# Order of a chunk pair's matmuls: high weights of both chunks, then low weights of both

## The chip, the cores and the metric

The kernel runs on one core of one Trainium2 chip. The metric is the device time of one execution in microseconds; lower is better.

## What is computed

Two transformer layers over 256 tokens of width 2048, all in float32. The first has sparse attention (compressed, selected and window branches, 16 heads in 4 groups) and a gated feed-forward of inner width 5632; the second has an mLSTM branch (8 heads), a pooling branch and a gated merge. Cut to the large products, with `@` a matrix product:

```python
h = x + nsa_mixer(rmsnorm(x, g0), ...)          # h @ w_in (q, k, v), attention, @ w_out
h = h + swiglu(rmsnorm(h, g1), w_in, w_out)     # (silu(a) * b) @ w_out
x = rmsnorm(h, g2)
proj = einsum('bsd,de->bse', _rmsnorm(x, w), w_in_2)   # q, k, v, o, z, gates, pool, merge gates
...                                             # causal conv, mLSTM, pooling
out = (sigmoid(g_a) * br_a + sigmoid(g_b) * br_b) @ w_out_2
x = x + _rmsnorm(out, norm_post_w)
```

Nearly all of the arithmetic is 256 rows times weight matrices. The weights are read once each, 387 MB in all.

## The kernel before

**Stream.** The weights lie in DRAM as 730 chunks of 128 partitions x 1024 floats (512 KB), in the order of use. Chunk c passes through slot c % 4 of a ring (`RING = 4`). SyncE loads it into `raw[slot]`. ScalarE (`split`, L435 to L442) copies it to `w_hl[slot][:, 0]` in the type fp32r, which keeps the high part of each number, and raises `hi_ready`. VectorE (`split`, L711 to L717) subtracts that from `raw` and writes the rest, the low part, to `w_hl[slot][:, 1]`, raising `lo_ready`. ScalarE may overwrite a slot only when TensorE has raised `chunks_done` for the chunk that was in it four chunks before. Both engines run three chunks ahead (`AHEAD = 3`).

**Products.** The activations are split in the same way (`x_hl`, `f_hl`, `o_hl`, `ya_hl`, `m_hl`: index 0 high, 1 low). A block of 512 output columns is two units, each of 256 columns with its own PSUM pair `sets[0]` or `sets[1]`. A unit is 4 chunks for an inner width of 2048 (`n // 2` with `n = NB = 8`), 11 for the second product of the feed-forward (`ND = 22`), 2 for the pooling branch's product. In `unit_features` (L1367) one chunk holds four 128-row tiles of the inner dimension by two of the output. Its first half are 8 matmuls of the high weights against high and low activations side by side, 512 columns each (L1373); its second half, behind a wait for `lo_ready`, are 8 matmuls of the low weights against the high activations, 256 columns each (L1378). `unit_tokens` (L1382) has the roles exchanged: it waits for `lo_ready` at its start, because its 8 matmuls of 512 columns (L1388) stream high and low weights side by side, and its 8 of 256 columns (L1391) need the high ones alone.

**Units and steps.** `gemm` (L1412) runs two units, `unit` (L1402) the chunks of one. `unit` also takes `steps`, small pieces of other work on TensorE that are put behind a chunk by its number within the block: the attention's score matmuls behind chunks 0, 2, 4, 6 and its value matmuls and transposes behind 1, 3, 5, 7 (`attention`, L1548); parts of the mLSTM heads (L1709 to L1713); row statistics (L1454). VectorE and ScalarE have such steps of their own between their `split`s, in the order in which the Python loops write them; each engine works in that order.

**Attention on TensorE.** `scores(gi, n)` (L1508) writes banks `m[0]` and `m[1]`. VectorE's `mask_scores` (L897) reads both, adds the bias, finds the maxima and raises `masked` with its last operation (L924). `values(gi, n)` (L1534) writes `m[1]` again, so it waits for the masks of the head two further on, which is the head whose scores stand behind the chunk just before:

```python
            if n + 2 < HPG:
                pe.wait_ge(masked, gi * HPG + (n + 3))
```

The groups gi = 0, 1, 2 run as `steps` of a `gemm` (L1563 to L1565). Group 3 runs in a loop over chunks of `block_features` (L1573), which doesn't go through `unit`.

**mLSTM heads.** In the block of the gate z (`ml_block(i, 5)`, L1712) TensorE sums squares of head 0 behind chunk 2 and of head 1 behind chunk 5 (`head_squares`, L1703). VectorE's order there is: low parts, `head_var(0)` (L1237) behind the split of the fourth turn, another split, `take_z` (L1260) at half, `head_sum(1)` (L1232), on which `head_squares(1)` waits. There are four such blocks (i = 0 to 3).

**Inputs of a block.** With `ready`, a chunk also waits until the activations that it reads are there: chunk j of the first unit waits for `x_ready` 4j + 4.

Of the kernel before, what the change touches and what calls it, by code (L numbers as in the profile page):

```python
# [13 lines left out]
P = 128  # L14
S = 256
# [19 lines left out]
HB, HT = BLK // 2, FT // 2  # L35
# [105 lines left out]
def program(nc, d):  # L141
# [108 lines left out]
    sets = [ctx.enter_context(nc.psum_tensor(f"set{n}", [P, 2 * BLK], F32)) for n in range(2)]  # L250
# [6 lines left out]
    hi_ready, lo_ready = sem("hi_ready"), sem("lo_ready")  # L257
    chunks_done = sem("chunks_done")
# [1068 lines left out]
    def _(pe):  # L1327
        mm = nc.tensor.matmul
# [38 lines left out]
        def unit_features(at, j, out, hl, kts, first):  # L1367

            w = w_hl[at.slot(j)]
            tiles = [(k, kt, f) for k, kt in enumerate(kts) for f in range(HT)]  # L1370
            for k, kt, f in tiles:
                c = slice(k * HB + f * P, k * HB + (f + 1) * P)
                mm(out[:, f * 2 * S:(f + 1) * 2 * S], w[:, 0, c], hl[:, kt, :, :], start=first and k == 0, stop=False,  # L1373
                   skip_group_check=True)
            pe.wait_ge(lo_ready, at.at(j) + 1)
            for k, kt, f in tiles:
                c = slice(k * HB + f * P, k * HB + (f + 1) * P)
                last = mm(out[:, f * 2 * S + S:(f + 1) * 2 * S], w[:, 1, c], hl[:, kt, 0, :], start=False, stop=True,  # L1378
                          skip_group_check=True)
            return last  # L1380

        def unit_tokens(at, j, out, hl, kts, first):  # L1382

            w = w_hl[at.slot(j)]
            tiles = [(k, kt, t) for k, kt in enumerate(kts) for t in range(TT)]
            pe.wait_ge(lo_ready, at.at(j) + 1)
            for k, kt, t in tiles:
                mm(out[:, t * 2 * HB:(t + 1) * 2 * HB], hl[:, kt, 0, t * P:(t + 1) * P], w[:, :, k * HB:(k + 1) * HB],  # L1388
                   start=first and k == 0, stop=False, skip_group_check=True)
            for k, kt, t in tiles:  # L1390
                last = mm(out[:, t * 2 * HB + HB:(t + 1) * 2 * HB], hl[:, kt, 1, t * P:(t + 1) * P],  # L1391
                          w[:, 0, k * HB:(k + 1) * HB], start=False, stop=True, skip_group_check=True)
            return last

        def chunk(at, j, wait, emit):

            pe.wait_ge(hi_ready, at.at(j) + 1)
            if wait:
                pe.wait_ge(*wait)
            emit().then_inc(chunks_done, 1)  # L1400

        def unit(at, j0, number, the_set, n, ready, hl, emit, steps):  # L1402

            await_set(number)
            for j in range(n):
                kts = range(4 * j, 4 * j + 4)
                chunk(at, j0 + j, ready(kts[-1]) if ready else None,
                      lambda: emit(at, j0 + j, sets[the_set % 2], hl, kts, j == 0))
                if steps and j0 + j in steps:
                    steps[j0 + j]()  # L1410

        def gemm(at, number, the_set, n=NB, ready=None, hl=x_hl, emit=(unit_features, unit_features), steps=None):  # L1412

# [38 lines left out]
        for n in range(4):  # L1452
            gemm(Pos(C_KV + n * NB), B_KV + 2 * n, B_KV, ready=operand_ready(0) if n == 0 else None,
                 steps={1: relative, 6: lambda: stats(0, 0, 1)} if n == 0 else None)  # L1454
        for n in range(2):
            await_set(B_KV + 8 + n)
            at = Pos(C_KV + (4 + n) * NB)
# [12 lines left out]
        for n in range(2):  # L1470
            await_set(B_CMP + n)
            out = sets[(B_CMP + n) % 2][0:GROUPS * NC, 0:2 * CH]
            at = Pos(C_CMP + n * NB)
            pe.wait_ge(blk_ready, n + 1)
            for j in range(NB):
                pe.wait_ge(lo_ready, at.at(j) + 1)
                w = w_hl[at.slot(j)]
                for k in range(4):
                    kt, c = 4 * j + k, slice(k * CH, (k + 1) * CH)
                    mm(out, blk_hi[:, n, kt, :], w[:, :, c], start=kt == 0, stop=False, skip_group_check=True)  # L1480
                    last = mm(out[:, CH:2 * CH], blk_lo[:, n, kt, :], w[:, 0, c], start=False, stop=kt == CB - 1,
                              skip_group_check=True)
# [89 lines left out]
        at, slot = Pos(C_OUT), 0  # L1572
        for block_no, j0, count in ((0, 0, 6), (1, 0, 6), (0, 6, 2), (1, 6, 2)):  # L1573
            for j in range(j0, j0 + count):
                kts = (2 * j, 2 * j + 1)
# [295 lines left out]
```

## Time and profile before

| | us |
|---|---|
| median of 3 runs | 2188.57 (2186.68 to 2189.26) |
| profiled execution | 2188.28 |
| its span, first to last instruction | 2186.6 |
| TensorE busy | 2159.9 (99%) |
| VectorE busy | 1414.4 (65%) |
| ScalarE busy | 1049.6 (48%) |
| DMA queue of the weights, share of 16 engines | 54.1% |

Between the span and the time of the same execution lie 1.7 us that no instruction covers. TensorE's duration of one matmul overlaps the next one's, so the pace is read from the starts: a row of the time line gives the start of a run of equal instructions, how long the run lasted and how many it has.

### The profile page before, as it was taken

To read this page: it belongs to the slowest core of one execution; us is meant where nothing else is said; L and a number is where in the kernel's file an instruction comes from. 1 tells how busy PE (TensorE), PEld (TensorE's weight loads), DVE (VectorE), ACT (ScalarE), POOL (GpSimd) and SP (SyncE) were. 2 spreads that over 40 slices of the span, in tenths; PEclk is the share of its full clock that TensorE was granted. 3 is DMA by queue.
4 is the path that set the end of the run, shared out by engine and by line. 5 is a ranking of instruction groups with operands and counts; after the bars stand their busy time and mean duration, and the time that the engine had idled before them with its cause. 6 is when DMAs were issued, how large, how long until landed. Compare 5 with 4: busy or idle time off the path is not lost.

```text
span 2186.6 us, 34436 instructions
## 1 busy us (share of the span) xinstructions
PE 2159.9 (99%) x12438; PEld 1891.5 (87%) x12438; DVE 1414.4 (65%) x1839; ACT 1049.6 (48%) x1373; POOL 70.5 (3%) x143
## 2 busy tenths in 40 slices
PE   9999999999999999999999999999999999999996
PEld 8877889888888888888888888888888888888885
DVE  7756664766666656655556677867777676566565
ACT  5445554454444444444444455444454454444453
POOL 1000322000000000000000000000000000000001
PEclk9999999999999999999999999999999999999998
DMA  7557333556565655555555456545555555555552
GB/s 277 185 189 244 117 127 117 179 172 200 180 196 178 195 188 186 190 190 187 188 190 191 145 174 193 180 168 184 187 177 177 171 185 190 184 192 189 186 191 97
DMA packets 108598, 395.54 MB, mean 181 GB/s; under 512 B 12307, under 2 KB 12323, under 8 KB 108513
## 3 DMA queue, kind: packets, MB, share of 16 engines
q1 hardware_dynamic: 106272, 386.97, 54.1%
q0 software_dynamic: 2096, 7.33, 1.0%
q8 instruction: 61, 1.00, 0.2%
q14 instruction: 25, 0.20, 0.0%
q10 hardware_dynamic: 144, 0.04, 0.0%
HBM read 389.83 MB, written 2.13 MB: 179 GB/s over the span
## 4 chain that ended last, share of the span: by engine, by line
PE 95%; DVE 1%; ACT 1%; DMA 1%; issue 0%; SPq 0%; POOL 0%; ACTq 0%
PE set L1373 52%; PE set L1378 27%; PE set L1388 4%; PE set L1391 2%; PE set L1362 1%; PE set L1364 1%; PE set L1363 1%; PE misc L1544 1%; ACT w_hl L442 1%; PE set L1348 1%; PE set L1350 1%; PE set L1349 1%; PE misc L1530 1%; DMA h<-in_x 0%; PE misc L1679 0%; PE misc L1546 0%
## 5 line engine op out<-in xcount | busy, mean ns | idle before, releaser
L717 DVE TENSOR_TENSOR w_hl<-raw,w_hl 128x1024 fp32r<-128x1024 f32 x730 | 888.0, 1225 | 586.0 <-ACT w_hl L442 579.0
L442 ACT ACTIVATE w_hl<-raw 128x1024 fp32r<-128x1024 f32 x730 | 762.2, 1055 | 799.9 <-PE set L1378 693.7
L1373 PE MATMUL set<-x_hl,w_hl 128*128 128x512 f32 x3584 | 908.1, 395 | 0.0
L1373 PEld LDWEIGHTS set<-x_hl,w_hl 128*128 128x128 f32 x3584 | 646.7, 189 | 118.7 <-issue 1.4
L1378 PEld LDWEIGHTS set<-x_hl,w_hl 128*128 128x128 f32 x3584 | 490.0, 191 | 35.4
L1378 PE MATMUL set<-x_hl,w_hl 128*128 128x256 f32 x3584 | 500.5, 283 | 0.0
L1373 PE MATMUL set<-f_hl,w_hl 128*128 128x512 f32 x704 | 176.3, 392 | 0.0
L449 ACT ACTIVATE cross<-set 128x512 f32<-128x512 f32 (+1 forms) x152 | 88.5, 583 | 138.2 <-PE set L1378 126.7
L1373 PEld LDWEIGHTS set<-f_hl,w_hl 128*128 128x128 f32 x704 | 126.6, 189 | 22.6
L1378 PEld LDWEIGHTS set<-f_hl,w_hl 128*128 128x128 f32 x704 | 96.0, 190 | 6.9
L1378 PE MATMUL set<-f_hl,w_hl 128*128 128x256 f32 x704 | 98.2, 282 | 0.0
L1388 PE MATMUL set<-w_hl,x_hl 128*128 128x512 f32 x384 | 96.2, 392 | 0.0
L1388 PEld LDWEIGHTS set<-w_hl,x_hl 128*128 128x128 f32 x384 | 69.1, 189 | 12.4
L1373 PE MATMUL set<-ya_hl,w_hl 128*128 128x512 f32 x256 | 64.1, 392 | 0.0
L1373 PE MATMUL set<-m_hl,w_hl 128*128 128x512 f32 x256 | 64.1, 392 | 0.0
L1391 PEld LDWEIGHTS set<-w_hl,x_hl 128*128 128x128 f32 x384 | 52.4, 190 | 3.7
L1391 PE MATMUL set<-w_hl,x_hl 128*128 128x256 f32 x384 | 53.5, 282 | 0.0
L1373 PEld LDWEIGHTS set<-ya_hl,w_hl 128*128 128x128 f32 x256 | 46.0, 189 | 8.2
L1373 PEld LDWEIGHTS set<-m_hl,w_hl 128*128 128x128 f32 x256 | 46.0, 189 | 8.2
L400 POOL TENSOR_TENSOR prob<-prob,share 128x128 f32<-128x128 f32 (+1 forms) x96 | 38.0, 428 | 115.0 <-DVE share L935 115.0
L1167 DVE SCALAR_TENSOR_TENSOR t<-cq,cur,t 128x256 f32<-128x256 f32 x96 | 40.0, 479 | 0.0
L526 ACT ACTIVATE prob<-prob,ntop 128x128 f32<-128x128 f32 (+1 forms) x96 | 37.4, 390 | 0.0
(294 smaller groups left out, 1764.0 us busy)
## 6 DMA issues: line engine op xcount, KB each, us to landing
raw<-in_weights SPq DMA_DIRECT2D x730, 512.0 KB, 4.1
bias_g<-bias POOLq DMA_DIRECT2D x4, 572.0 KB, 3.8
cur<-in_cur POOLq DMA_DIRECT2D x4, 535.0 KB, 3.9
h<-in_x SPq DMA_DIRECT2D x4, 512.0 KB, 8.4
bias<-u_dram POOLq DMA_DIRECT2D x1, 2048.0 KB, 14.4
out<-y_t SPq DMA_DIRECT2D x4, 512.0 KB, 2.8
w<-in_w POOLq DMA_DIRECT2D x1, 256.0 KB, 6.6
vm<-in_causal POOLq DMA_DIRECT2D x1, 192.0 KB, 3.1
```

The costliest lines, as they stand in the source:

```text
L400: last = g.tensor_tensor(pr[:, lo:lo + w], pr[:, lo:lo + w], sh[:, b, t:t + 1].to_broadcast([P, w]), ALU.mult)
L442: a(w_hl[at.slot(j)][:, 0, :], raw[at.slot(j)][:, :], ACT.Copy).then_inc(hi_ready, 1)
L449: a(dst, src, ACT.Copy).then_inc(crossed, 1)
L526: last = a(pr[:, lo:lo + w], pr[:, lo:lo + w], ACT.Exp, bias=ntop[:, b, t:t + 1], accum_out=total[n % 2][:, b, t:t + 1])
L717: tt(w_hl[s][:, 1, :], raw[s][:, :], w_hl[s][:, 0, :].bitcast(F32), ALU.subtract).then_inc(lo_ready, 1)
L1167: last = stt(t1[:, f, :], cq[:, f, k:k + S], cur[:, c + k:c + k + 1], t1[:, f, :], ALU.mult, ALU.add)
L1348: mm(o, w[:, 0, c], hl[:, kt, 0, :], start=starts, stop=False, skip_group_check=True)
L1349: mm(o, w[:, 0, c], hl[:, kt, 1, :], start=False, stop=False, skip_group_check=True)
L1373: mm(out[:, f * 2 * S:(f + 1) * 2 * S], w[:, 0, c], hl[:, kt, :, :], start=first and k == 0, stop=False, skip_group_check=True)
L1378: last = mm(out[:, f * 2 * S + S:(f + 1) * 2 * S], w[:, 1, c], hl[:, kt, 0, :], start=False, stop=True, skip_group_check=True)
L1388: mm(out[:, t * 2 * HB:(t + 1) * 2 * HB], hl[:, kt, 0, t * P:(t + 1) * P], w[:, :, k * HB:(k + 1) * HB], start=first and k == 0, stop=Fals ...
L1391: last = mm(out[:, t * 2 * HB + HB:(t + 1) * 2 * HB], hl[:, kt, 1, t * P:(t + 1) * P], w[:, 0, k * HB:(k + 1) * HB], start=False, stop=Tru ...
```

## The change

The two halves of a chunk become two functions, `high` and `low`. `unit` takes its chunks in pairs: the high halves of both, then the low halves of both. A chunk's `chunks_done` and its step come after its own low half. A unit of 11 chunks has five pairs and a single one. The number and kind of matmuls stay; each chunk keeps its waits for `hi_ready`, `ready` and `lo_ready`, ahead of the half that needs them. (In `unit_tokens` the wait for `hi_ready` is gone, that for `lo_ready` stays.) `block_features`, `block_tokens`, `narrow` and the compression loop are as before.

```diff
--- before.py
+++ after.py
@@ -1368,29 +1368,42 @@
 
             w = w_hl[at.slot(j)]
             tiles = [(k, kt, f) for k, kt in enumerate(kts) for f in range(HT)]
-            for k, kt, f in tiles:
-                c = slice(k * HB + f * P, k * HB + (f + 1) * P)
-                mm(out[:, f * 2 * S:(f + 1) * 2 * S], w[:, 0, c], hl[:, kt, :, :], start=first and k == 0, stop=False,
-                   skip_group_check=True)
-            pe.wait_ge(lo_ready, at.at(j) + 1)
-            for k, kt, f in tiles:
-                c = slice(k * HB + f * P, k * HB + (f + 1) * P)
-                last = mm(out[:, f * 2 * S + S:(f + 1) * 2 * S], w[:, 1, c], hl[:, kt, 0, :], start=False, stop=True,
-                          skip_group_check=True)
-            return last
+
+            def high():
+                pe.wait_ge(hi_ready, at.at(j) + 1)
+                for k, kt, f in tiles:
+                    c = slice(k * HB + f * P, k * HB + (f + 1) * P)
+                    mm(out[:, f * 2 * S:(f + 1) * 2 * S], w[:, 0, c], hl[:, kt, :, :], start=first and k == 0, stop=False,
+                       skip_group_check=True)
+
+            def low():
+                pe.wait_ge(lo_ready, at.at(j) + 1)
+                for k, kt, f in tiles:
+                    c = slice(k * HB + f * P, k * HB + (f + 1) * P)
+                    last = mm(out[:, f * 2 * S + S:(f + 1) * 2 * S], w[:, 1, c], hl[:, kt, 0, :], start=False, stop=True,
+                              skip_group_check=True)
+                last.then_inc(chunks_done, 1)
+
+            return high, low
 
         def unit_tokens(at, j, out, hl, kts, first):
 
             w = w_hl[at.slot(j)]
             tiles = [(k, kt, t) for k, kt in enumerate(kts) for t in range(TT)]
-            pe.wait_ge(lo_ready, at.at(j) + 1)
-            for k, kt, t in tiles:
-                mm(out[:, t * 2 * HB:(t + 1) * 2 * HB], hl[:, kt, 0, t * P:(t + 1) * P], w[:, :, k * HB:(k + 1) * HB],
-                   start=first and k == 0, stop=False, skip_group_check=True)
-            for k, kt, t in tiles:
-                last = mm(out[:, t * 2 * HB + HB:(t + 1) * 2 * HB], hl[:, kt, 1, t * P:(t + 1) * P],
-                          w[:, 0, k * HB:(k + 1) * HB], start=False, stop=True, skip_group_check=True)
-            return last
+
+            def high():
+                pe.wait_ge(lo_ready, at.at(j) + 1)
+                for k, kt, t in tiles:
+                    mm(out[:, t * 2 * HB:(t + 1) * 2 * HB], hl[:, kt, 0, t * P:(t + 1) * P], w[:, :, k * HB:(k + 1) * HB],
+                       start=first and k == 0, stop=False, skip_group_check=True)
+
+            def low():
+                for k, kt, t in tiles:
+                    last = mm(out[:, t * 2 * HB + HB:(t + 1) * 2 * HB], hl[:, kt, 1, t * P:(t + 1) * P],
+                              w[:, 0, k * HB:(k + 1) * HB], start=False, stop=True, skip_group_check=True)
+                last.then_inc(chunks_done, 1)
+
+            return high, low
 
         def chunk(at, j, wait, emit):
 
@@ -1402,12 +1415,18 @@
         def unit(at, j0, number, the_set, n, ready, hl, emit, steps):
 
             await_set(number)
-            for j in range(n):
-                kts = range(4 * j, 4 * j + 4)
-                chunk(at, j0 + j, ready(kts[-1]) if ready else None,
-                      lambda: emit(at, j0 + j, sets[the_set % 2], hl, kts, j == 0))
-                if steps and j0 + j in steps:
-                    steps[j0 + j]()
+
+            for pair in range(0, n, 2):
+                js = range(pair, min(pair + 2, n))
+                parts = [emit(at, j0 + j, sets[the_set % 2], hl, range(4 * j, 4 * j + 4), j == 0) for j in js]
+                for j, (high, low) in zip(js, parts):
+                    if ready:
+                        pe.wait_ge(*ready(4 * j + 3))
+                    high()
+                for j, (high, low) in zip(js, parts):
+                    low()
+                    if steps and j0 + j in steps:
+                        steps[j0 + j]()
 
         def gemm(at, number, the_set, n=NB, ready=None, hl=x_hl, emit=(unit_features, unit_features), steps=None):
```

## Rows read from the trace of the kernel before

**Rows 1.** The page: TensorE's busy time, and the ending chain by line
```profile
PE 2159.9 (99%) x12438; PEld 1891.5 (87%) x12438; DVE 1414.4 (65%) x1839; ACT 1049.6 (48%) x1373; POOL 70.5 (3%) x143
...
PE set L1373 52%; PE set L1378 27%; PE set L1388 4%; PE set L1391 2%; PE set L1362 1%; PE set L1364 1%; PE set L1363 1%; PE misc L1544 1%; ACT w_hl L442 1%; PE set L1348 1%; PE set L1350 1%; PE set L1349 1%; PE misc L1530 1%; DMA h<-in_x 0%; PE misc L1679 0%; PE misc L1546 0%
```

**Rows 2.** Waits: engine, line, releaser; total us, times, longest us
```profile
PE misc L1530 <- POOL prob L400: 1.8, 1, 1.8
PE misc L1446 <- DVE stat L778: 1.5, 1, 1.5
...
PE set L1373 <- ACT w_hl L442: 0.2, 1, 0.2
...
ACT w_hl L442 <- PE set L1378: 693.7, 427, 7.0
```

**Rows 3.** Time line of TensorE, one chunk: start, us, engine, line, operation, count
```profile
1003.16 2.00 PE L1373 MATMUL set<-f_hl,w_hl 128*128 128x512 f32 x8
1005.00 1.12 PE L1378 MATMUL set<-f_hl,w_hl 128*128 128x256 f32 x8
1005.95 2.00 PE L1373 MATMUL set<-f_hl,w_hl 128*128 128x512 f32 x8
```

**Rows 4.** Time line of TensorE in a block of `block_tokens`, 512-column matmuls alone
```profile
138.44 0.39 PE L1362 MATMUL set<-w_hl,x_hl 128*128 128x512 f32 x1
...
143.20 0.39 PE L1362 MATMUL set<-w_hl,x_hl 128*128 128x512 f32 x1
```

**Rows 5.** Time line, fourth chunk of the mLSTM part's first block
```profile
1180.44 3.50 DVE L717 TENSOR_TENSOR w_hl<-raw,w_hl 128x1024 fp32r<-128x1024 f32 x3 [2.93 <-ACT w_hl L442]
...
1181.93 2.00 PE L1388 MATMUL set<-w_hl,x_hl 128*128 128x512 f32 x8
```

**Rows 6.** Time line, the first chunk of the kernel
```profile
9.48 2.07 PE L1373 MATMUL set<-x_hl,w_hl 128*128 128x512 f32 x8
...
10.49 1.69 DVE L747 SCALAR_TENSOR_TENSOR x_hl<-h,gains,x_hl 128x256 fp32r<-128x256 f32 x4 [0.27 <-ACT x_hl L465]
...
11.40 1.11 PE L1378 MATMUL set<-x_hl,w_hl 128*128 128x256 f32 x8
```

**Rows 7.** Stretches: us, busy PE, PEld, DVE, ACT, POOL, PEclk, DMA share, GB/s
```profile
28.00:33.00 5.00, 3.46 (x22) 2.95 (x20) 4.90 (x6) 3.20 (x3) 0.00 (x0) 1.00 0.87 320
33.00:36.50 3.50, 3.50 (x11) 2.76 (x11) 3.35 (x4) 0.08 (x1) 0.00 (x0) 0.53 1.01 369
...
220.00:224.00 4.00, 2.18 (x14) 1.94 (x15) 3.97 (x5) 2.59 (x6) 3.68 (x5) 1.00 0.30 116
```

**Rows 8.** Time line, attention group 1: behind the scores of one head
```profile
246.63 2.09 PE L1373 MATMUL set<-x_hl,w_hl 128*128 128x512 f32 x8
...
247.02 0.25 DVE L910 TENSOR_TENSOR prob<-misc,bias_g 128x15 f32<-128x15 f32 x2
...
248.56 1.11 PE L1378 MATMUL set<-x_hl,w_hl 128*128 128x256 f32 x8
248.63 0.64 DVE L924 TENSOR_SCALAR ntop<-top 128x6 f32<-128x6 f32 x1
...
249.51 0.59 PE L1544 MATMUL misc<-prob_t,v_g 128*128 128x256 f32 x2
```

**Rows 9.** The last operation of the masks: duration ns min/median/max, starts
```profile
L924 DVE TENSOR_SCALAR ntop<-top x16: 172/514/640, 212.0 to 358.0; 128x6 f32<-128x6 f32 x16
```

**Rows 10.** Time line, block of the gate z, i = 1
```profile
1460.94 0.60 PE L1707 MATMUL misc<-t,ones 128*128 128x256 f32 x2
...
1462.23 1.23 DVE L717 TENSOR_TENSOR w_hl<-raw,w_hl 128x1024 fp32r<-128x1024 f32 x1 [2.29 <-ACT w_hl L442]
...
1463.83 1.75 DVE L1240 RECIPROCAL stat<-stat 128x256 f32<-128x256 f32 x1
...
1467.92 0.42 DVE L1235 TENSOR_TENSOR t<-t 128x256 f32<-128x256 f32 x1
...
1469.75 0.60 PE L1707 MATMUL misc<-t,ones 128*128 128x256 f32 x2
```

## Prediction

> **What bounds the kernel now.** I read the page first: TensorE is busy for 2159.9 of 2186.6 us, and the chain that ended last runs through its two matmul lines, L1373 and L1378, for 79% of the span [rows 1]. So the kernel is bound by TensorE's stream, and there are three ways to change its time: the pace inside the stream, the few holes in it, and new holes. The waits come second. TensorE's own are few: 1.8 us for the probabilities of the first head, 1.5 us for the first row statistics, 0.2 us at one chunk of the out projection [rows 2]. ScalarE waits for TensorE 427 times, 693.7 us in all [rows 2]; the splits are far ahead, held back by the ring. The time line comes third. A chunk is 8 matmuls of 512 columns in 1.84 us (1003.16 to 1005.00) and 8 of 256 in 0.95 us, 2.79 us together [rows 3]. I call them the high and the low run.
>
> **Pace of the stream.** In `block_tokens`, where only 512-column matmuls follow each other, 21 of them take 4.76 us (138.44 to 143.20), 0.2267 us each, with chunk waits between them [rows 4]. At that pace 8 take 1.813 us; the high run takes 1.84 [rows 3]. So a high run that follows a low run has about 0.027 us that a high run behind another high run should not have. The low run doesn't show such an excess: 0.95 us for 8, 0.119 each. Rounding is 0.01 us on each side, and a long low run may be slower by that much a pair. I take 0.02 us saved per pair, between 0.027 and 0.017. The units have 680 chunks, of which 8 are the single last chunks of units of 11; 336 pairs. 336 x 0.02 = 6.7 us gained (5.7 to 9.1; 0 if the excess doesn't hang on the change of width, and then the low run's loss of up to 3.4 us is left).
>
> The Trainium skill says otherwise ("TensorE: Matmul & The Clock Gate", Back-to-back issue gap): the gap of warm matmuls hangs on their columns alone, N/2.4 + 2.5 ns. By it the order is worth nothing, and the sum below would be 6.7 us higher; rows 3 against rows 4, 230 ns and 227 ns for the same 512 columns, don't agree with it.
>
> **The ring.** The first chunk of a pair now reports `chunks_done` one high run, 1.84 us, later, so its successor in the slot is split later by that; the second reports as before, but its high run is wanted one low run, 0.95 us, earlier. From a chunk's report to the use of its successor in the slot are three chunks, 8.4 us [rows 3]; a split takes 1.2 us on VectorE [rows 5, 10], about as much ahead of it on ScalarE, and ScalarE has idle time of its own, 1.6 us per wait (693.7 us over 427) [rows 2]. Some 5 us of room hide 1.84 and 0.95. SyncE's loads wait for `lo_ready`, which is early too. Zero, save where a split is late today:
> - The out projection's chunk with the 0.2 us wait [rows 2] is the fourth of its block, the second of a pair. Its split comes when it came; TensorE asks 0.95 us sooner: +0.9 us.
> - The fourth chunk of the mLSTM part is of `unit_tokens`, whose high run needs the low part. VectorE ends the first of three splits at 1180.44 + 1.17 = 1181.61, TensorE starts at 1181.93 [rows 5]. Wanted 0.95 us sooner, at 1180.98, it comes 0.63 us late, and I add 0.15 for the semaphore and the weight load: +0.8 us.
> - At the start, the second chunk needs the second four activation tiles, ready at 10.49 + 1.69 = 12.18; the first high run ends at 11.40 [rows 6]. Today the low run lies between: 0.78 us and a weight load, +0.85 us.
>
> **Steps behind odd-numbered chunks** (the second of a pair) keep their place. Those behind even-numbered ones move behind the partner's high run, 1.84 us later. For a step that waited this is a gain: the row statistics stand behind chunk 6, and their wait of 1.5 us [rows 2] is covered if VectorE's squares don't move as much. VectorE is busy for 4.90 of the 5 us before them [rows 7], so it is late by its own work and not for TensorE's reports; I take the whole 1.5. After that wait TensorE's granted clock fell, 0.53 on average over 33.0 to 36.5 [rows 7], its lower level of 1.2 GHz for most of the stretch, which costs 3.5 x 0.47 = 1.6 us. I count it as gone with the gap ahead of it: together -3.1 us (0 at worst).
>
> **Attention, the largest term.** `scores(n)` is behind an even-numbered chunk, `values(n - 2)` behind the odd one next to it, and values wait for the masks of head n, made from those scores (both use bank `m[1]`). Today a high and a low run lie between scores and values; after the change only the low run. The row: the high run behind the scores starts at 246.63, VectorE begins the masks at 247.02 and ends them at 248.63 + 0.64 = 249.27; the values start at 249.51 [rows 8]. So the masks end 2.64 us after TensorE has left the scores, and the cover is 2.88 us, hardly more. With a low run alone it is 0.95 us, plus about 0.08 for the change from the scores' operand type, which the high run shows here (1.93 us, 246.63 to 248.56, instead of 1.84). The wait in this head is 2.64 + 0.1 (weight load ahead of the matmul, estimated) - 1.03 = 1.7 us; its last operation took 0.64 us where the median of 16 is 0.51 [rows 9], so I take 1.6 for the mean head. No other work is behind the wait but the transposes and the next pair, all on TensorE. How many: groups 1 and 2 have four each, group 0 the last two (its first slots have no head to finish), group 3 runs outside `unit`. 10 x 1.6 = 16 us lost; with the shortest and the longest of that operation, 0.17 and 0.64, 10 x 1.25 to 10 x 1.7. VectorE can't start sooner, because the scores are later by the same 1.84 us, and what it does in between was done before them. The next exponentials start behind transposes, as today. The only wait for the probabilities now is that of the first head [rows 2], and that chain isn't lengthened, so nothing further adds.
>
> **The gate z's blocks.** `head_squares(0)` is behind chunk 2 and moves 1.84 us. `head_var(0)` on VectorE is also behind the low part of chunk 6, which waits for chunk 2's `chunks_done`. Today that split starts at 1462.23, `head_var` ends at 1463.83 + 1.75 = 1465.58, then follow a split and `take_z`, `head_sum(1)` ends at 1467.92 + 0.42 = 1468.34, and TensorE takes it at 1469.75, 1.4 us later [rows 10]. The chain begins with chunk 2's report and is back to back but for short gaps, so it moves by nearly the whole 1.84 us, to about 1470.2, while TensorE arrives when it did, 1469.7 with the faster runs: with the weight load a wait of 0.7 us in each of the 4 blocks, 2.8 us (0 where the gaps take up the shift, 5 at twice 0.7). Behind it are only TensorE's own matmuls.
>
> **Sum.** -6.7 - 3.1 + 0.85 + 0.9 + 0.8 + 16 + 2.8 = +11.5 us. On the profiled execution's 2188.28 us, of which 1.7 lie outside the span, that is 2199.8; the median of the runs is 0.3 higher: 2200.
>
> **Rivals.**
> - *Clock drops* (chance 0.14). The new holes are 1.6 us, ten of them 11 us apart. One hole of 1.5 us was followed by a stretch at half clock; the one of 1.8 us in the first attention group was not, the granted clock is 1.00 over 220 to 224 [rows 7]. If four of the ten cost 1.6 us each, the time is 2206; if all, 2216.
> - *The excess of the high run stays* (0.14). It may belong to the place of the weights in the chunk and not to the change of width; rows 4 are another kind of block, which speaks for this. Then 6.7 us of gain are missing, and up to 3.4 us are lost on the low runs: 2207 to 2210. The rule of the skill's page named above, by which no order of matmuls costs more than another, ends at the lower of the two, 2207.
> - *The masks are hidden after all* (0.08; the other side). If TensorE's queue delays the low run, or VectorE ends the masks 1.6 us sooner, the 16 us vanish. Then -9.8 + 2.55 + 2.8 = -4.5 us is left: 2184, faster. It decides at a masks' time of 1.04 us behind the scores, against 2.64 measured; nothing in the rows speaks for it but that the profile shows ends of matmuls by a model. Half way the result is no change, 2189 to 2193 (0.10).
> - My forecast, 2195 to 2204: 0.54.
>
> The range leaves out the faster case (0.08), the lower part of the half way (0.03) and the far part of the clock's and of the second rival's (0.07): 2190 to 2210. A measurement of this kernel can tell about 0.2%, 4.4 us. Chances: slower by more 0.82, within it 0.10, faster 0.08.
>
> **What would show it.** In the profile after, the waits of TensorE should have a new row, L1544's operation released by VectorE's L924, ten times, 1.6 us at most each; without it the largest term is wrong. The row for the first statistics should be gone, and the clock at full speed behind it. Four waits on L1235 of about 0.7 us should be at the squares of the second head. The time line of a pair in the feed-forward should show 16 matmuls of 512 columns in about 3.66 us and 16 of 256 in 1.91, 5.57 together instead of 5.59. A longer low run, or a high run of 3.68, would show the second rival. Half-clock stretches between 230 and 330 us would show the first.

## The result and the profile after

The changed kernel takes 2196.2 us (median of 7 runs, 2193.51 to 2198.64); the kernel before, timed beside it, 2187.9 (7 runs, 2185.85 to 2189.27). The ratio is 1.0039, with a 95% interval of 1.0029 to 1.0049: slower by 8.3 us. The forecast was 2200.0 with a range of 2190 to 2210, and slower. The profiled execution took 2196.38 us.

The page of the kernel after: span, busy time of the engines, and the chain that ended last by line, which answers to [rows 1].

```profile
span 2193.9 us, 34360 instructions
...
PE 2154.9 (98%) x12438; PEld 1891.1 (86%) x12438; DVE 1392.9 (63%) x1839; ACT 1031.4 (47%) x1373; POOL 70.9 (3%) x143
...
PE set L1376 52%; PE set L1383 26%; PE set L1397 4%; PE set L1402 2%; DVE w_hl L717 1%; PE misc L1563 1%; ACT w_hl L442 1%; PE set L1362 1%; PE set L1363 1%; PE set L1364 1%; PE set L1348 1%; PE set L1350 1%; PE set L1349 1%; PE misc L1549 1%; PE misc L1698 0%
```

The high and low runs are L1376 and L1383 now (L1373 and L1378 before). TensorE is busy for 5.0 us less and the span is 7.3 us longer: the stream got shorter, and holes were added. Which ones, the waits of TensorE say (line, releaser; total us, times, longest), against [rows 2]:

```profile
PE misc L1563 <- DVE ntop L924: 8.4, 9, 1.0
...
PE set L1376 <- DVE x_hl L747: 1.5, 1, 1.5
PE misc L1726 <- DVE t L1235: 1.3, 4, 0.4
...
PE set L1376 <- ACT w_hl L442: 1.2, 1, 1.2
PE set L1376 <- DVE t L1078: 1.1, 1, 1.1
PE misc L1563 <- issue: 1.0, 1, 1.0
PE misc L1549 <- POOL prob L400: 0.8, 1, 0.8
...
PE set L1397 <- DVE w_hl L717: 0.7, 1, 0.7
```

L1563 is the first value matmul of a head (L1544 before). It waits ten times; nine are put down to the masks, the tenth, which is the first in time, to "issue", for which the profile names no releaser; its masks end 0.15 us ahead of it. The 1.5 us of the first row statistics are gone. A wait on L1078 is there that the prediction doesn't have.

One head of attention group 1 in the time line, which answers to [rows 8]:

```profile
245.02 1.11 PE L1383 MATMUL set<-x_hl,w_hl 128*128 128x256 f32 x8
...
245.82 2.25 POOL L400 TENSOR_TENSOR prob<-prob,share 128x128 f32<-128x128 f32 x6 [6.72 <-DVE share L935]
...
247.25 1.19 PE L1383 MATMUL set<-x_hl,w_hl 128*128 128x256 f32 x8
247.53 0.25 DVE L910 TENSOR_TENSOR prob<-misc,bias_g 128x15 f32<-128x15 f32 x2 [1.80 <-PE misc L1539]
...
249.14 0.17 DVE L924 TENSOR_SCALAR ntop<-top 128x6 f32<-128x6 f32 x1
...
249.37 0.70 PE L1563 MATMUL misc<-prob_t,v_g 128*128 128x256 f32 x2 [0.93 <-DVE ntop L924]
```

Only the low run at 247.25 lies between the scores and the values. The masks start 0.28 us behind the scores and end at 249.31; TensorE stands idle for 0.93 us.

Pairs in the feed-forward's second product, which answer to [rows 3]:

```profile
999.83 2.08 PE L1383 MATMUL set<-f_hl,w_hl 128*128 128x256 f32 x16
1001.74 3.82 PE L1376 MATMUL set<-f_hl,w_hl 128*128 128x512 f32 x16
1005.39 2.08 PE L1383 MATMUL set<-f_hl,w_hl 128*128 128x256 f32 x16
1007.31 3.82 PE L1376 MATMUL set<-f_hl,w_hl 128*128 128x512 f32 x16
```

A pair is 5.57 us (1001.74 to 1007.31). By the starts in nanoseconds its median is 5567 (3654 high, 1912 low, over 246 pairs); a chunk of the kernel before is 2793 (1841 and 952, over 548), two of them 5586. A pair saves 19 ns.

The place of every microsecond comes from the times at which TensorE reports the same chunk in both traces (the last matmul of a chunk). The table gives, for each stretch, the kernel's duration less that of the kernel before, in us. x1 to x8 are the experiments below, without x4, which leaves work out.

| stretch | after | x1 | x2 | x3 | x5 | x6 | x7 | x8 |
|---|---|---|---|---|---|---|---|---|
| chunks 1 and 2 | +0.91 | -0.11 | +1.08 | +0.85 | +0.13 | +0.92 | -0.09 | +0.15 |
| chunks 3 to 16 (first statistics) | -3.52 | -1.63 | -3.52 | -3.52 | -3.37 | -3.52 | -1.63 | -3.45 |
| rest of keys and values | -0.16 | 0 | -0.16 | -0.16 | 0 | -0.16 | 0 | -0.16 |
| compression, first block of queries | +0.22 | +0.78 | +0.34 | +0.13 | -0.43 | -0.01 | -0.88 | -0.04 |
| attention group 0 | +0.14 | +0.01 | +0.31 | +0.25 | 0 | +0.14 | -1.05 | +0.32 |
| groups 1, 2, and the step behind 2's last chunk | +10.48 | 0 | 0 | +1.66 | 0 | +10.52 | 0 | 0 |
| out projection, third block | +0.94 | 0 | +0.93 | +0.94 | 0 | +0.93 | 0 | 0 |
| out projection, fourth block | -0.08 | 0 | -0.08 | -0.08 | 0 | -0.08 | 0 | -0.08 |
| feed-forward, first product | -1.76 | -1.76 | -1.76 | -1.76 | 0 | -1.76 | +14.61 | -1.76 |
| feed-forward, second product | -0.80 | -0.80 | -0.80 | -0.80 | 0 | -0.80 | -0.80 | -0.80 |
| mLSTM i = 0, first block | +0.87 | 0 | +0.88 | +0.88 | 0 | +0.87 | 0 | 0 |
| its second block | +0.85 | 0 | +0.85 | +0.87 | 0 | +0.85 | 0 | 0 |
| its next three | -0.23 | 0 | +1.40 | -0.25 | -1.51 | +1.42 | 0 | +1.37 |
| its gate z | +0.57 | 0 | +0.57 | +0.57 | 0 | 0 | 0 | 0 |
| i = 1 to 3 | +0.33 | 0 | +0.33 | +0.33 | 0 | -1.20 | 0 | -1.24 |
| merge, last product | -1.44 | -1.44 | -1.44 | -1.44 | 0 | -1.44 | -1.44 | -1.44 |

Where pairs alone act, the table is -0.020 us for each: 1.76 over 88, 1.12 over 56. The first row also holds the moment at which TensorE begins, which differs between traces by more than 0.1 us. Groups 1 and 2 of attention lose 4.66 and 4.63 us for four waits each (the rest of 10.48 is the step behind group 2's last chunk): with 0.08 for their four pairs, 1.19 a wait. (The profile's 0.9 to 1.0 counts only from the modelled end of the matmul before, and the end overlaps the next start.)

### The profile page after: what moved, and what is told of

Its sections match the earlier page's. It is cut to its first block, busy times and chain, and to the rows that moved or that the text cites. A ratio compares the mean times of both kernels' runs of the same rounds, so it can differ in the third digit from the quotient of the medians.

```text
span 2193.9 us, 34360 instructions
## 1 busy us (share of the span) xinstructions
PE 2154.9 (98%) x12438; PEld 1891.1 (86%) x12438; DVE 1392.9 (63%) x1839; ACT 1031.4 (47%) x1373; POOL 70.9 (3%) x143
## 4 chain that ended last, share of the span: by engine, by line
PE 94%; DVE 3%; ACT 1%; issue 1%; DMA 1%; POOL 0%; SPq 0%; DVEq 0%; ACTq 0%
PE set L1376 52%; PE set L1383 26%; PE set L1397 4%; PE set L1402 2%; DVE w_hl L717 1%; PE misc L1563 1%; ACT w_hl L442 1%; PE set L1362 1%; PE set L1363 1%; PE set L1364 1%; PE set L1348 1%; PE set L1350 1%; PE set L1349 1%; PE misc L1549 1%; PE misc L1698 0%
## 5 line engine op out<-in xcount | busy, mean ns | idle before, releaser
L717 DVE TENSOR_TENSOR w_hl<-raw,w_hl 128x1024 fp32r<-128x1024 f32 x730 | 876.2, 1225 | 671.0 <-ACT w_hl L442 666.2
L442 ACT ACTIVATE w_hl<-raw 128x1024 fp32r<-128x1024 f32 x730 | 745.9, 1056 | 894.7 <-PE set L1383 798.3
L1376 PE MATMUL set<-x_hl,w_hl 128*128 128x512 f32 x3584 | 861.6, 392 | 2.6 <-DVE x_hl L747 1.5
L1376 PEld LDWEIGHTS set<-x_hl,w_hl 128*128 128x128 f32 x3584 | 659.9, 188 | 133.2 <-DVE x_hl L747 2.8
L1383 PEld LDWEIGHTS set<-x_hl,w_hl 128*128 128x128 f32 x3584 | 462.1, 191 | 18.4 <-issue 0.7
L1383 PE MATMUL set<-x_hl,w_hl 128*128 128x256 f32 x3584 | 472.3, 284 | 0.0
L1376 PE MATMUL set<-f_hl,w_hl 128*128 128x512 f32 x704 | 168.7, 391 | 0.0
L1376 PEld LDWEIGHTS set<-f_hl,w_hl 128*128 128x128 f32 x704 | 129.1, 188 | 24.8
L1383 PEld LDWEIGHTS set<-f_hl,w_hl 128*128 128x128 f32 x704 | 90.8, 191 | 3.7
L1397 PE MATMUL set<-w_hl,x_hl 128*128 128x512 f32 x384 | 91.8, 391 | 0.7 <-DVE w_hl L717 0.7
L1383 PE MATMUL set<-f_hl,w_hl 128*128 128x256 f32 x704 | 91.9, 283 | 0.0
L1376 PE MATMUL set<-ya_hl,w_hl 128*128 128x512 f32 x256 | 61.1, 391 | 0.0
L1376 PE MATMUL set<-m_hl,w_hl 128*128 128x512 f32 x256 | 61.1, 391 | 0.0
L1376 PEld LDWEIGHTS set<-m_hl,w_hl 128*128 128x128 f32 x256 | 47.1, 188 | 9.1
L1376 PEld LDWEIGHTS set<-ya_hl,w_hl 128*128 128x128 f32 x256 | 47.1, 188 | 9.1
L400 POOL TENSOR_TENSOR prob<-prob,share 128x128 f32<-128x128 f32 (+1 forms) x96 | 37.0, 418 | 117.6 <-DVE share L935 117.6
```

What stands on the lines that cost most here:

```text
L400: last = g.tensor_tensor(pr[:, lo:lo + w], pr[:, lo:lo + w], sh[:, b, t:t + 1].to_broadcast([P, w]), ALU.mult)
L442: a(w_hl[at.slot(j)][:, 0, :], raw[at.slot(j)][:, :], ACT.Copy).then_inc(hi_ready, 1)
L717: tt(w_hl[s][:, 1, :], raw[s][:, :], w_hl[s][:, 0, :].bitcast(F32), ALU.subtract).then_inc(lo_ready, 1)
```

## The experiments

Two theories stood against each other behind the sum. Mine: the change is a small uniform gain of the stream (0.02 us a pair) plus a few holes, each at one named step that lost its cover. The rival: the order of the halves costs or gives something everywhere (through the ring, the pace, the clock), and the named steps are a part of it only. The kernel before took 2186.95 us beside x1 to x4 (27 runs) and 2186.87 beside x5 to x8 (10 runs).

**Pairs only where no step stands between** (x1). `unit` gets its group size as a parameter, 1 by default; 2 in both products of the feed-forward, the merge and the last product, 200 pairs.

```diff
-            for pair in range(0, n, 2):
-                js = range(pair, min(pair + 2, n))
+            for pair in range(0, n, group):
+                js = range(pair, min(pair + group, n))
```

> Pairs only in blocks without steps between chunks: the feed-forward's two products, the merge and the last projection, 200 pairs; every other unit takes its chunks one by one as before. Theory (a high run behind another high run lacks the excess of 0.027 us, the low run loses about 0.007): 200 x 0.02 = 4.0 us faster than before, 2184, no wait in TensorE's list that before doesn't have. Rival (the order of matmuls is worth nothing, the time by columns alone): the time of before, 2188. Second rival (the ring has less room and costs something): slower than before.

Measured: 2184.74 us (11 runs), ratio to before 0.9989 (0.9980 to 0.9998). In the trace the four stretches are shorter by 1.76, 0.80, 1.12 and 0.32, 4.00 in all, and no wait came with them: TensorE's wait for the statistics is as before. So this part of the change alone makes the kernel faster. The medians differ by 2.2 us where 4.0 was expected; the interval reaches from 0.4 to 4.4. The clock brought what the prediction didn't have (columns as in [rows 7]):

```profile
28.00:33.00 5.00, 3.52 (x22) 3.02 (x21) 4.90 (x7) 3.09 (x3) 0.00 (x0) 1.00 0.86 279
33.00:36.50 3.50, 3.50 (x20) 3.03 (x20) 3.18 (x3) 0.25 (x1) 0.00 (x0) 1.00 1.02 369
165.00:170.00 5.00, 3.14 (x15) 1.97 (x14) 2.78 (x3) 4.33 (x6) 0.00 (x0) 0.83 0.80 259
```

The same hole of 1.5 us is there (TensorE busy for 3.52 of the 5 us), and the granted clock behind it is 1.00, not 0.53; a lower one stands at 165 us instead, where the kernel before has none.

**Attention chunk by chunk, the rest as in the change** (x2): `group=1` in the two calls of `gemm` that carry the attention's steps.

> The changed kernel, but in the three blocks that carry the attention's steps the chunks run one by one. Theory (the attention's waits on the masks are the bulk of the loss): the nine waits on L924 are gone, 10.9 us less than the changed kernel, 2185, which is 2 to 3 us below before. Rival (the time was lost all over, through the ring): at most 2 us less than the changed kernel, 2194.

Measured: 2186.97 us (10 runs), ratio 0.9997 (0.9987 to 1.0006). All waits on L924 are gone, and groups 1 and 2 take what they took before, to 0.01 us. So the attention's waits account for the slowdown of the whole kernel. The expectation of 2 to 3 us below before is not borne out by the medians, which are equal; the interval reaches from 2.8 us below to 1.3 above.

**A head's scores one run earlier** (x3). In the attention's blocks the step of a pair's first chunk stands behind that chunk's high run; the partner's high run and the low run then lie between scores and values again.

```diff
                     high()
+                    if j0 + j in early:
+                        steps[j0 + j]()
...
-                    if steps and j0 + j in steps:
+                    if steps and j0 + j in steps and j0 + j not in early:
```

> The changed kernel, but in the attention blocks the step of a pair's first chunk runs behind its high run instead of its low run. Between scores and values then lie a high and two low runs, 3.7 us, against masks of 1.8 to 2.6 us. Theory (it is the distance from scores to values that costs): no wait on L924, about 10.9 us less than the changed kernel, 2185, equal to the single chunks within 0.5 us. Rival (the waits come from less room in the ring or from VectorE's work between): waits on L924 stay and the time is over 2190.

Measured: 2187.39 us (10 runs), ratio 1.0000 (0.9991 to 1.0010). Two rows of its waits, and its row for the last operation of the masks, which answers to [rows 9]:

```profile
PE misc L1539 <- DVE q_t L790: 1.0, 1, 1.0
...
PE misc L1539 <- DVE o_hl L947: 0.5, 3, 0.2
...
L924 DVE TENSOR_SCALAR ntop<-top x16: 172/335/656, 209.6 to 357.2; 128x6 f32<-128x6 f32 x16
```

No wait for the masks is left, though the attention still runs in pairs. It is the distance between scores and values that counts, as the prediction had it, not the pairs as such. The scores now sometimes stand too early for their own operands. The wait on L790 is in group 0; groups 1 and 2, with the step behind them, lose 1.66 us in place of 10.48, of which 0.5 are the three waits on L947 and the rest stays open.

**The kernel before, with five of POOL's six scalings of a head left out** (x4; the probabilities are then not all scaled). It asks what holds back the masks' last operation.

```diff
-                for b, t, lo, w in ((1, 0, O_SEL, P), (1, 1, O_SEL + P, S), (0, 0, O_CMP, NC),
-                                    (0, 1, O_CMP + 16, NC), (2, 0, O_WIN, P), (2, 1, O_WIN + P, S)):
+                for b, t, lo, w in ((0, 1, O_CMP + 16, NC),):
```

> The kernel before, with five of the six multiplications left out by which POOL scales each head's probabilities (so the output isn't the reference's). Theory (VectorE's L924 waited until POOL's multiplications had ended, as it ends 0.03 us behind them in every head): L924 takes 0.17 us in all heads instead of 0.51 in the median, the masks end 2.15 us after the scores instead of 2.5, and the first head's wait of TensorE, 1.8 us, is gone; 2186. Rival (L924 waits for its own operand on VectorE): L924 stays at 0.5 us.

Its lines are one lower from there on: L923 is L924, L399 is L400.

```profile
L923 DVE TENSOR_SCALAR ntop<-top x16: 171/172/175, 209.8 to 353.8; 128x6 f32<-128x6 f32 x16
...
L399 POOL TENSOR_TENSOR prob<-prob,share x16: 203/214/216, 216.3 to 362.0; 128x15 f32<-128x15 f32 x16
```

The operation takes 0.17 us in all 16 heads; [rows 9] has 0.51 for the median. So its length was a wait for POOL. By the single records of the kernel before, it ends 0.03 us behind POOL's last multiplication in 14 heads; in the second head it takes 0.27 us and ends 0.03 us behind the fifth of six. So it waits for the one multiplication that is running, 0.2 to 0.6 us long, and not for all of them. (The first head has none beside it. TensorE's wait for the first head's probabilities, 1.8 us in [rows 2], is gone with it; its one execution took 2184.14 us.) In the head of [rows 8] this row of the kernel before says the same:

```profile
247.00 2.24 POOL L400 TENSOR_TENSOR prob<-prob,share 128x128 f32<-128x128 f32 x6 [6.99 <-DVE share L935]
```

POOL ends at 249.24, the masks' last operation at 249.27. After the change POOL starts 1.4 us ahead of the later scores (245.82 against 247.25 above), is done by 248.07, and the operation takes 0.17. The Trainium skill ("SBUF — State Buffer", Who interferes with whom) counts `tensor_scalar`, which L924 is, among the operations that can take the port pair that VectorE and GpSimd share, and has one engine block while the other holds it. Both rows agree.

**The kernel before with the statistics one chunk later** (x5).

```diff
-                 steps={1: relative, 6: lambda: stats(0, 0, 1)} if n == 0 else None)
+                 steps={1: relative, 7: lambda: stats(0, 0, 1)} if n == 0 else None)
```

> The kernel before, with one edit: the first row statistics stand behind chunk 7 instead of chunk 6. No chunk runs in pairs. If the 1.5 us by which TensorE waited there were work of VectorE that comes when it comes, the chunk of 2.79 us between hides it: the wait's row is gone and the eighth chunk's report comes 1.5 us sooner. If VectorE's squares moved with TensorE, the wait would stay. On the clock: if the hole alone calls the half-clock stretch behind it, the clock is 1.00 from 28 to 40 us and the gain is 3.1 us; if it comes in either case it is at another place in that part of the kernel, and the gain is 1.5.

Measured: 2183.11 us, one execution. The wait is gone, and chunks 3 to 16 take 3.37 us less, where x1, with the hole but with full clock, takes 1.63 less. The difference, 1.7 us, is the hole with what is beside it; the 1.63 is the clock, since x1 has full speed there where before has not. The second gain of 1.51 us, in the mLSTM part, is also the clock: at the same place the kernel before is granted 0.83 over 10 us.

```profile
28.00:33.00 5.00, 5.00 (x30) 4.37 (x29) 4.90 (x6) 3.25 (x3) 0.00 (x0) 1.00 0.93 314
33.00:36.50 3.50, 3.50 (x23) 3.11 (x22) 3.42 (x4) 0.09 (x2) 0.00 (x0) 1.00 1.01 366
1235.00:1245.00 10.00, 10.00 (x61) 8.86 (x59) 7.36 (x13) 5.10 (x6) 0.00 (x0) 1.00 0.37 128
```

This edit has nothing to do with the mLSTM part, 1200 us later. So neither stretch at half clock can be put down to an edit from one trace of each kernel. Its time from one execution is not a measurement of the 1.5 us. The four timed executions of the kernel before with the same mean clock, 0.997, took 2183.6 to 2185.4 us.

**The gate z chunk by chunk, the rest as in the change** (x6): `group=1` in that call.

> The kernel after, with the four blocks of the gate z chunk by chunk again. My theory: their squares of head 1 wait because the report of chunk 2 comes 1.84 us later. Then the waits on L1235 are gone and each of the four blocks is 0.59 us shorter (0.67 for the wait and its weight load, less 0.08 for the four pairs given up), 2.3 us together. The rival: the wait comes from the other pairs ahead of the block, which shift VectorE's work; then waits of about 0.3 us stay and the blocks only get longer by 0.08 each.

Measured: 2195.78 us, one execution. No wait on L1235 is left. The first gate z is 0.58 us shorter than in the kernel after (+0.57 to 0), those of i = 1 to 3 1.53 together (+0.33 to -1.20), 2.1 us in all. Expected were 2.3. My account held. The +1.42 in "its next three" is once more half clock that this trace has and that of after has less of.

**Groups of four** (x7): x1, with `group=4` in the first product of the feed-forward.

> Pairs only where no step stands between them (first product of the feed-forward, second product, merge, last product), and in the first product of the feed-forward, 176 chunks, groups of four: four high runs, then four low runs. If what a pair saves is the one change from 256 to 512 columns, at 0.020 us, four chunks have one change instead of two: the first product is 44 x 0.02 = 0.9 us shorter than with pairs, 2.6 us shorter than before. The rival is the ring: the first chunk's report comes 5.5 us later than chunk by chunk, and its successor is wanted 2.9 us after it; a high split on ScalarE takes 1.06 us, so the high runs shouldn't wait, but if loads or VectorE's low parts come late, waits on L442 or L717 appear and the stretch is longer than with pairs.

Measured: 2197.03 us, one execution; that product takes 14.6 us more than before, 16.4 more than with pairs. The rival was right. The wait, and the time line around one of the twelve:

```profile
PE set L1376 <- ACT w_hl L442: 12.5, 12, 1.8
...
569.40 2.98 ACT L442 ACTIVATE w_hl<-raw 128x1024 fp32r<-128x1024 f32 x3 [6.69 <-PE set L1383]
...
572.08 5.63 PE L1376 MATMUL set<-x_hl,w_hl 128*128 128x512 f32 x24
...
576.71 1.06 ACT L575 ACTIVATE f_hl<-f_b 128x1024 f32 x1 [3.75 <-DVE f_b L1020]
577.67 1.04 ACT L442 ACTIVATE w_hl<-raw 128x1024 fp32r<-128x1024 f32 x1
...
578.76 2.11 PE L1376 MATMUL set<-x_hl,w_hl 128*128 128x512 f32 x8 [1.05 <-ACT w_hl L442]
```

ScalarE gets three slots from 569.40 on and splits them. Before the fourth its program puts the output of the block just finished (L575), which waits 3.75 us for VectorE; the fourth split ends at 578.71, and TensorE has run out after three high runs. Such a group takes 12.43 to 13.34 us. My expectation counted the split's 1.06 us and not what stands ahead of it. The pace is as expected only in part: of 43 groups 21 take 11.113 us from high run to high run, against 11.134 for two pairs, a further 0.021 for one change of width less; twelve have the wait, and the other ten take 11.13 without one, which stays open.

x7 is x1 word for word up to the feed-forward, and still it differs in the first head of attention. Two rows of x1, then two of x7:

```profile
217.50 3.31 POOL L400 TENSOR_TENSOR prob<-prob,share 128x128 f32<-128x128 f32 x6 [18.86 <-DVE share L935]
...
219.12 2.77 DVE L717 TENSOR_TENSOR w_hl<-raw,w_hl 128x1024 fp32r<-128x1024 f32 x2
```

```profile
215.85 2.25 POOL L400 TENSOR_TENSOR prob<-prob,share 128x128 f32<-128x128 f32 x6 [18.86 <-DVE share L935]
...
217.47 3.05 DVE L717 TENSOR_TENSOR w_hl<-raw,w_hl 128x1024 fp32r<-128x1024 f32 x2
```

By the single records five of the six multiplications are alike. The last begins 0.02 us behind VectorE's split (L717) in both. In x1 it takes 1.66 us and the split 1.21; in x7 it takes 0.61 and the split 1.71. So either can be the one that is held, and TensorE waits 1.8 us in x1 and 0.8 in x7. The kernel before, x2, x5 and x8 have it as x1.

The same 1.0 us is in the comparison of before and after (1.8 in [rows 2], 0.8 above), but there it comes another way:

```profile
215.91 2.25 POOL L400 TENSOR_TENSOR prob<-prob,share 128x128 f32<-128x128 f32 x6 [16.98 <-DVE share L935]
216.46 0.25 DVE L910 TENSOR_TENSOR prob<-misc,bias_g 128x15 f32<-128x15 f32 x2 [0.64 <-PE misc L1539]
...
218.44 2.71 DVE L717 TENSOR_TENSOR w_hl<-raw,w_hl 128x1024 fp32r<-128x1024 f32 x2
```

After the change the scores come later, so the masks begin 0.55 us behind POOL's start, and POOL is done at 218.16, before the split begins. That speaks for the 1.0 us being a gain of the change that the prediction doesn't have; no run tests it by itself, and x7 shows that the old order sometimes has it too.

**Pairs wherever they brought no wait** (x8): 292 pairs, and the statistics as in x5. The first block, the attention, the third block of the out projection, the gate z and the first two blocks of mLSTM i = 0 go chunk by chunk.

```diff
-                 steps={1: relative, 6: lambda: stats(0, 0, 1)} if n == 0 else None)
+                 steps={1: relative, 7: lambda: stats(0, 0, 1)} if n == 0 else None,
+                 group=1 if n == 0 else 2)
...
-            gemm(Pos(C_OUT, n, NB), B_OUT + 2 * n - 2, B_OUT, hl=o_hl)
+            gemm(Pos(C_OUT, n, NB), B_OUT + 2 * n - 2, B_OUT, hl=o_hl, group=n - 1)
-                 ready=operand_ready(2 * KT) if first else None, steps={5: norms} if first else None)
+                 ready=operand_ready(2 * KT) if first else None, steps={5: norms} if first else None, group=1 if first else 2)
```

> Pairs wherever no wait came from them: the two feed-forward products, merge, last product, the second to fourth blocks of keys and values, the first block of queries, the fourth of the out projection, and the mLSTM blocks other than the gate z's (in i = 0 not its first two), 292 pairs. Chunk by chunk: first block, attention, third block of the out projection, gate z. The first row statistics stand behind chunk 7. Theory: every pair is worth 0.020 us whatever stands between, and the waits come only from the five places named: 5.8 + 1.5 = 7.3 us below before, ratio 0.9967, about 2179.6 on a median of 2187. The rival, that each step between pairs costs something of its own, ends at pairs in the plain blocks alone, 4.0 + 1.5 = 5.5 us below, or worse.

Measured: 2179.96 us (6 runs, 2179.41 to 2181.96), ratio 0.9970 (0.9957 to 0.9982): 6.9 us below before, where 7.3 was expected, and by the two ratios some 15 below the kernel after. Its span, and its waits at the stream's lines and in attention:

```profile
span 2179.5 us, 34360 instructions
...
PE misc L1553 <- POOL prob L400: 1.8, 1, 1.8
...
PE set L1376 <- ACT w_hl L442: 0.2, 1, 0.2
```

These are the waits of [rows 2], without that for the statistics. The lower rival, 5.5 us or less, lies inside the interval of 3.9 to 9.4 us; it is the trace that speaks against it, where the 60 pairs of i = 1 to 3, many of them around steps, save their 0.02 us as well (-1.24). This is the version to keep. Attention group 0 is 0.3 us longer in x8 and x2, which have in common that the block ahead of it is in pairs; that was not followed up.

## Why the prediction was right, and where not

The sign came out, 8.3 us slower where 11.5 were forecast, and the time is inside the likeliest case's 2195 to 2204. By the steps:

**Pairs, -6.7: right.** 0.020 us each in every stretch where nothing else changed. The excess does sit at the change of width. The first five starts of a high run behind a low run are 6, 9, 1, 6 and 4 ns beyond the 227 of the later ones, 26 in all, and positions 9 to 16 of a long run have 227 flat; the first two of a low run behind a high run are 7 and 1 ns short of the 120 of the others. One change forth and one back is 26 - 8 = 18 ns. The rival that it belongs to the place in the chunk is out. So, for this stream, is the reading of the Trainium skill's formula that the prediction weighed, by which no order would matter; the section gives that formula for an isolated matmul, which this stream doesn't test.

**Attention, +16: right mechanism, size too large.** Ten waits on L924 came, as said, and x2 and x3 tie them to the attention and to the distance from scores to values. The term that was mis-sized is the masks' time, and with it the 1.6 us a wait. The prediction took the 2.64 us from scores to masks' end as VectorE's own work. In the kernel before, 0.39 of it were the start and 0.47 the hold by POOL (0.64 less 0.17). After the change the start is 0.28 and the hold is gone in that head, 2.06 us in all; with the prediction's own formula that is 2.06 + 0.1 - 1.03 = 1.1 us, and 1.19 is what a wait costs. 10 x 1.19 = 11.9. The bounds given for the operation, 0.17 to 0.64, did contain this; the choice of the median was the error, since the length of an operation of 128x6 elements that takes 0.17 in one head and 0.64 in another is a wait and moves with the order.

**First statistics, -3.1: half of it shown.** The wait of 1.5 us is gone, in after and in x5. The other 1.6 were called the clock's and tied to the hole ahead of it. The profiled execution of after has no hole and full clock there:

```profile
28.00:33.00 5.00, 5.00 (x29) 4.35 (x28) 4.36 (x6) 1.73 (x2) 0.00 (x0) 1.00 0.94 342
33.00:36.50 3.50, 3.50 (x24) 3.15 (x23) 2.65 (x4) 2.34 (x2) 0.00 (x0) 1.00 1.01 365
1240.00:1250.00 10.00, 10.00 (x46) 8.36 (x45) 6.62 (x13) 2.18 (x3) 0.00 (x0) 0.83 0.47 157
```

But so have x1, x4 and x7 from 28 to 40 us, with the hole. The step "I count it as gone with the gap ahead of it" failed: of the four traces with the hole only one has the half clock behind it, so the hole alone doesn't bring it. The -3.5 of the table agrees with the -3.1 by luck for half of it. The timed runs show no gain of clock either: its mean over a run is 0.994 to 0.997 in the 37 of the kernel before that stand beside the experiments, and 0.994 to 0.996 in the 7 of the kernel after.

**Start +0.85: right** (+0.91 in the table; the wait on L747 is 1.5 us, as TensorE also began earlier, at 8.64). **Out projection +0.9: right**, 0.94 + 0.08 for its pairs; its wait went from 0.2 to 1.2 us. **Fourth chunk of mLSTM +0.8: right**, 0.87 + 0.09. The three are the same working: a time at which an operand is there, and a time at which it is now wanted.

**Gate z +2.8: right mechanism, somewhat too large.** The rows of i = 1, against [rows 10]:

```profile
1470.77 0.60 PE L1726 MATMUL misc<-t,ones 128*128 128x256 f32 x2
...
1473.65 1.75 DVE L1240 RECIPROCAL stat<-stat 128x256 f32<-128x256 f32 x1
...
1477.72 0.42 DVE L1235 TENSOR_TENSOR t<-t 128x256 f32<-128x256 f32 x1
...
1478.20 0.70 PE L1726 MATMUL misc<-t,ones 128*128 128x256 f32 x2 [0.31 <-DVE t L1235]
```

From the first squares to the end of L1235 are 7.37 us (7.40 before): the chain moved whole, as said. The wait is 0.31, and with what stands around it each block costs 0.57 + 0.08 = 0.65, or 0.59 in i = 1 to 3; 2.4 us in all.

**Missed: the second block of mLSTM i = 0, +0.85.** The prediction looked for VectorE chains that begin with an even-numbered chunk's report only in the gate z's block. There is one more:

```profile
1205.29 1.23 DVE L717 TENSOR_TENSOR w_hl<-raw,w_hl 128x1024 fp32r<-128x1024 f32 x1 [2.81 <-ACT w_hl L442]
...
1211.02 0.69 DVE L1078 TENSOR_TENSOR t<-t,rms 128x512 f32<-128x512 f32 x1
1211.76 2.56 PE L1376 MATMUL set<-x_hl,w_hl 128*128 128x512 f32 x10 [1.13 <-DVE t L1078]
```

The split at 1205.29 refills the slot of the block's chunk 6, the first of a pair. Behind it stand the second variance with its reciprocal and the two takes, up to L1078, which frees the bank that the next block writes. Before the change that chain ended at 1202.88, 0.34 us ahead of TensorE's start; it moved by 1.6 us against TensorE, and 1.1 of wait came. A wait of 0.4 us that before had in the same block (L1618, for L1082) is gone, so the block costs 0.85 + 0.08.

**The sum.** -6.7 - 3.4 (the table's 3.52 without its seven pairs) + 0.9 + 1.0 + 1.0 + 11.9 + 2.4 + 0.9 = +8.0. With -1.0 from the first head, and +0.4 in the compression, which goes either way from trace to trace (-1.06 to +0.60 in the experiments), that is +7.4; the spans differ by 7.3. The 4 us by which 11.5 was too high are the size of the attention's error (16 to 11.9), but that is in part luck: the second block's +0.9, which was missed, and the first head's -1.0, which was missed too, cancel. And 1.6 of the gain is the half clock that the profiled execution of before happened to have.

**The rivals.** Clock drops did not come: no stretch of after between 220 and 330 us is below full speed, with ten holes of 0.9 to 1.0 us in it. Masks hidden after all, and the excess stays: neither.

## What to carry to other kernels

A reordering inside a saturated stream is worth what its own rows say, here 0.02 us a pair; the price is at the steps whose cover it takes. List every step that waits, and every chain on another engine that begins with a report that the reordering delays, and work out for each when the operand is there and when it is now wanted. Then apply the order only where the list is empty: in 292 places, with one step moved by a chunk, the kernel gained 6.9 us; in all 336 it lost 8. And before a duration is used in such a sum, look at its smallest value over the trace: where one short operation takes three times that, it is waiting, and the wait may not survive the reordering.

## What the runs showed of the hardware that was not expected

- A VectorE operation of 128x6 elements takes 0.17 us alone and up to 0.66 beside POOL's multiplications; it ends 0.03 us behind the one that is running, and the next can start behind it. The other operations of the masks, one of whose operands is in PSUM, ran beside POOL at their usual length (0.28 and 0.42 in both time lines).
- Stretches at half clock wander from execution to execution of nearly the same program: at 33 us in the profiled before, at 168 us in x1, at none of these in x5; around 1240 us in nine of the ten traces, in x5 not at all, and twice as long in x2, x6 and x8 (0.66 over 1230 to 1240 in x8) as in the others. Each costs 1.6 to 1.7 us, twice that when long.
- It goes the other way too: where a multiplication of POOL and a split of VectorE (128x1024) began 0.02 us apart, the multiplication took 1.66 us instead of 0.61 in x1, and in x7, of the same code up to there, the split took 1.71 instead of 1.21.
- The change from 256 to 512 columns costs 26 ns over the first five matmuls, and that back gives 8; in the same stream 512 columns take 227 ns and 256 take 120.
